# Where two weight conversions stand in the first layer's feed-forward down-projection

## What is computed

```python
FF_HIDDEN = 2816                      # D_MODEL = 1024, SEQ = 512, CTX_LEN = 256

def swiglu(h, w_i, w_o):
    g, u = jnp.split(h @ w_i, 2, axis=-1)
    return (jax.nn.silu(g) * u) @ w_o

# in second_block, for layer l, with_ctx = l < 1
xl = xl + ml[5] * rms_norm(swiglu(adaln(xl, g[2], ml[3], ml[4]), w_ffn_in[l], w_ffn_out[l]), g[3])
if with_ctx:
    xc = xc + mc[5] * rms_norm(swiglu(adaln(xc, g[2], mc[3], mc[4]), w_ffn_in[l], w_ffn_out[l]), g[3])
```

## Time and profile before

| | |
|---|---|
| median of three runs | 3219.26 us |
| profiled execution: span from first to last instruction | 3213.4 us |
| instructions in it | 44931 |
| TensorE matmul busy | 2931.1 us (91%) |
| VectorE busy | 1629.9 us (51%) |
| ScalarE busy | 1040.4 us (32%) |
| mean granted TensorE clock | 0.959 of full |

### The profile page before, as it was taken

One profiled execution on the slowest core, in us unless ns is written; L12 is line 12 of the kernel. 1 busy time (PEld: TensorE's weight loads), 2 busy tenths in 40 slices (PEclk: granted clock), 3 DMA queues, 4 the chain that ended last, 5 costly groups with the idle time before them and its releaser, 6 DMA issues.

```text
span 3213.4 us, 44931 instructions
## 1 busy us (share of the span) xinstructions
PE 2931.1 (91%) x18762; PEld 2400.9 (75%) x18762; DVE 1629.9 (51%) x3421; ACT 1040.4 (32%) x2010; POOL 208.6 (6%) x270
## 2 busy tenths in 40 slices
PE   8988999999999998888799999999899797899998
PEld 6766788888977566677568888888666686578886
DVE  4333544445445255677763433333825667654444
ACT  3223433233343245343242211211415444332222
POOL 0000000000000100100000000000211246100001
PEclk9999999999999999899899999999999798899999
DMA  7434312222222110222512212121011110223221
GB/s 234 151 111 156 103 53 60 60 60 60 73 86 105 53 33 1 83 80 80 192 59 92 66 53 66 53 77 65 36 52 33 30 41 1 92 92 105 92 96 62
DMA packets 227830, 248.75 MB, mean 77 GB/s; under 512 B 5569, under 2 KB 193069, under 8 KB 226093
## 3 DMA queue, kind: packets, MB, share of 16 engines
q1 hardware_dynamic: 227628, 245.89, 23.8%
HBM read 236.43 MB, written 9.44 MB: 77 GB/s over the span
## 4 chain that ended last, share of the span: by engine, by line
PE 56%; DVE 9%; ACT 4%; issue 2%; DMA 1%; POOL 0%; ACTq 0%; SPq 0%; DVEq 0%; POOLq 0%
PE PS L2176 52%; PE PS L2180 2%; PE PS L2386 1%; ACT AR L179 1%; DVE AR L3153 1%; ACT L174 1%; DVE STAT L3089 1%; DMA WR<-in_w_in 1%; DVE AR L2898 1%; ACT EX L179 0%; DVE AR L2913 0%; DVE EX L3140 0%; DMA WR<-in_w_mod 0%; DVE AR L2909 0%; ACT STAT L179 0%
## 5 line engine op out<-in xcount | busy, mean ns | idle before, releaser
L2176 PE MATMUL PS<-HI,WC 128*128 128x512 f32 (+2 forms) x1600 | 428.0, 353 | 0.6 <-DVE WC L3134 0.6
L2176 PE MATMUL PS<-AR 128*64 128x64 f32 (+8 forms) x3756 | 315.7, 268 | 65.5 <-ACT AR L179 24.9
L2176 PE MATMUL PS<-DW,DH 128*128 128x384 f32 (+1 forms) x1344 | 355.4, 346 | 1.0 <-ACT DH L179 1.0
L2176 PEld LDWEIGHTS PS<-AR 128*64 128x64 f32 (+5 forms) x3756 | 270.7, 171 | 111.9 <-issue 33.8
L179 ACT ACTIVATE AR<-PS 128x512 f32<-128x512 f32 (+4 forms) x389 | 165.9, 453 | 552.6 <-PE PS L2176 428.2
L2176 PEld LDWEIGHTS PS<-HI,WC 128*128 128x128 f32 x1600 | 284.0, 189 | 42.5 <-DVE WC L3134 1.1
L2176 PE MATMUL PS<-LO,WC 128*128 128x512 f32 (+2 forms) x800 | 282.2, 353 | 0.0
L2176 PE MATMUL PS<-HT,WR 128*128 128x256 f32 (+1 forms) x928 | 261.4, 435 | 15.1 <-ACT EX L179 5.7
L2176 PE MATMUL PS<-WR,HT 128*128 128x128 f32 (+2 forms) x1296 | 252.0, 352 | 11.7 <-ACT AR L179 5.4
L2176 PEld LDWEIGHTS PS<-DW,DH 128*128 128x128 f32 x1344 | 240.6, 191 | 9.7 <-issue 7.1
L179 ACT ACTIVATE EX<-PS 128x256 f32<-128x256 f32 (+2 forms) x158 | 67.7, 431 | 530.6 <-PE PS L2176 530.6
(11 more groups left out here) (444 smaller groups left out, 4991.7 us busy)
## 6 DMA issues: line engine op xcount, KB each, us to landing
WR<-in_w_ffn_in SPq DMA_DIRECT2D x40, 1024.0 KB, 6.5
WR<-in_w_in_b SPq DMA_DIRECT2D x51, 512.0 KB, 6.0
WR<-in_w_mod SPq DMA_DIRECT2D x12, 2048.0 KB, 8.1
WR<-in_w_mod SPq DMA_DIRECT2D x24, 1024.0 KB, 5.3
WR<-in_w_ffn_out SPq DMA_DIRECT2D x22, 1024.0 KB, 4.9
WR<-in_w_in SPq DMA_DIRECT2D x40, 512.0 KB, 5.2
WR<-in_w_out SPq DMA_DIRECT2D x8, 2048.0 KB, 12.3
WR<-in_w_in SPq DMA_DIRECT2D x4, 2048.0 KB, 7.7
```

What stands on the lines that cost most here:

```text
L2176: mm = lambda o, l, r, start, stop: e.o.matmul(o, l, r, start=start, stop=stop, skip_group_check=True)
```

## The change

In layer 0 (`both`), a `down` step with c = 0 issues no conversion any more. A `down` step with c = 1 issues two: one ahead of its first group, as before, and one ahead of group i = 3. The order of the conversions among themselves, their buffers and their transfers stay. Steps `up` and all of layer 1 stay as they were. This concerns the ten pairs of blocks 0 to 9. Block 10's down-projection stands in another branch, in which nothing changes; its own two weight conversions are issued in the pair of block 9, and so are among the moved ones.

```diff
@@ -2100,11 +2100,15 @@
             convert(*work[3])
-            at_ = 4
+            next_at = [4]
+            def convert_next():
+                next_at[0] += 1
+                if next_at[0] <= len(work):
+                    convert(*work[next_at[0] - 1])
             for kind, b, c in sched[2:]:
-                if kind != "act" and at_ < len(work):
-                    convert(*work[at_])
-                    at_ += 1
+                turns = () if kind == "act" else (0,) if kind == "up" or not both else ((), (0, 3))[c]
+                if 0 in turns:
+                    convert_next()
                 if kind == "up":
...
                     for i in range(nt):
+                        if i and i in turns:
+                            convert_next()
                         down(i, c, b, o, ready, ac, an)
```

## The result

The changed kernel took 3201.36 us in the median of six runs (3200.87 to 3207.97), the kernel before 3218.44 us in the median of six (3212.48 to 3229.38). The ratio is 0.9946, with a 95% interval from 0.9933 to 0.9959: it is faster, by 17.1 us between the medians. I had forecast 12.0 us less and 3202.3 to 3213.3. The direction is right, but the time lies 0.9 us under the range, so the forecast missed. What follows shows that the pairs gave the 12 us to the tenth, and that the gain comes back to about 12 us when both kernels are run more often.

The account below looks back on a forecast made before the run. TensorE, waiting for VectorE's sums, was taken to bound the ten pairs. A gain of 1.28 less 0.08 us a pair, times ten, is 12.0: 3219.3 - 12.0 = 3207.3 us, range 3202.3 to 3213.3.

Parts of the forecast that it names:

- What bounds the stretch: Ten pairs, 1768 to 2253 us: TensorE sets the time, busy 476.85 of 485 us; weight loads waited 22.3 for VectorE's sums.
- The rule for VectorE's queue: Pricing of orders in the pairs: next VectorE instruction starts 0.60, 0.33 or 1.14 us on; a group costs about 1.365.
- The first half, 8.67 us: Pair's first half without its conversion: 8.19 + 0.12 + 0.37 us, groups 5 and 6 late; gain 1.28.
- The second, 8.35: Pair's second half with two conversions: 8.19 us plus 0.08 for each, a loss of 0.08.
- What else moves: Around the moved conversions: weights done before the up-projection at 1887.3, ScalarE's copies not late, no transfer issued by them.
- The sum of 12.0 us: Ten pairs: 1.28 - 0.08 = 1.20 us gained for each, 12.0 in all.
- the median of the runs is 5.86 above the span, so 3219.3 - 12.0: Whole kernel: profiled span 3213.4 us, run median 5.86 above it, so the forecast time is 3207.3.
- may move the time by 2 or 3 us: Behind the pairs: shifts of a few low-clock stretches either way, 2 or 3 us, counted in the range.
- Only the first wait goes: Rival, first half: later waits stay at 0.16, 0.16 and 0.37 us; gain 9 us, 3210.3; chance 0.09 (within 0.3%).
- No overlap on VectorE in the new order: Rival: VectorE's instructions take whole durations (0.69, 0.42, 1.23); gain 0.34 us a pair, 3.4 in all, 3215.9; chance 0.05.
- The change does nothing: Rival: waits set by something ending together with the sums, the conversion only cover; 3219 us, chance 0.03.
- Slower through the clock: Rival, behind 2253: low-clock time of about 103 us grows by 43 to about 146, ending 9.7 us (0.3%) slower; chance 0.02.

Follow-up runs that it names:

- six other orders: The change; both conversions opening the second half; both in the first; the first's behind the gating; gating spread alone; gating spread with conversions moved: 3201.36, 3214.26, 3224.69, 3206.03, 3211.20, 3199.94 us.
- The half-changed kernel: The change in the pairs of blocks 0 to 4 alone, against the kernel before: 3209.70 us against 3215.62, ratio 0.9983.
- both repeated comparisons: The changed kernel, unedited, run twice more against the kernel before: 3205.25 us against 3215.62, ratio 0.9959; 3204.82 against 3217.38, ratio 0.9958.
- the spread gating: Gating pieces behind groups 1, 3, 5 of the first half and 1 of the second, conversions ahead of second-half groups 3 and 6, against the kernel before: 3199.94 us, ratio 0.9948.

## Why the prediction was right and wrong

*What bounds the stretch: right.* TensorE, and VectorE's sums where it waits. Matmul waits for them vanished together with the subtraction ahead of the first sum.

*The rule for VectorE's queue: right.* Its constants were read from the order before (51.52), so that one is no test. For six other orders it gave pairs of 50.32 (the change), 51.4, 52.59, 50.5, 51.16 and 49.76; measured 50.32, 51.38, 52.59, 50.46, 51.17 and 49.80. The half-changed kernel mixes two of them: 50.92 on average, measured 50.91.

*The first half, 8.67 us: right*, 8.63 measured, group 5 and 6 late as said. *The second, 8.35: right*, 8.34, with a wait of 0.21 on the loads behind each conversion. *What else moves: right*; ScalarE's copies were done before VectorE asked.

*The sum of 12.0 us: right for the pairs*, and over all runs (12.7 between the medians of 38 and 17; 12.0 is 0.37% of 3217, inside the intervals of both repeated comparisons, 0.25 to 0.56% and 0.29 to 0.54%, though not of the first, 0.41 to 0.67%).

*The step that failed is the baseline and the scatter round it*: "the median of the runs is 5.86 above the span, so 3219.3 - 12.0", and with it "may move the time by 2 or 3 us". I took 5.86 us for what lies around the span. In the changed kernel's profiled execution it is 3206.71 - 3205.4 = 1.3, and in every run that lists both it is 1.3 to 1.4. So the profiled execution of before had itself taken about 3214.7 us, and the median of three stood 4.6 us above it: that was the size of the scatter, read as a constant. Sets of six differ by nearly as much (3201.36 and 3205.25 for the same changed kernel). The time came out 5.9 us under the forecast of 3207.3, and three parts add up to that: the baseline was 1.9 us too high (3219.26 against 3217.36, the median of 38), the gain over all runs is 0.7 more than 12.0, and the first six runs of the changed kernel lie 3.3 under the median of its 17. Most of the miss is therefore the luck of a set of three and a set of six. What the prediction did wrong was to allow 2 or 3 us for it, where executions of one kernel spread over 14 and medians of six differ by 4. With 1.3 us in place of 5.86 the same sum gives 3202.7. That is nearer to this set of six, but by luck again: the one profiled execution (3214.7) lies further from 3217.36 than the median of three does.

*The rivals.* Only the first wait goes: no. The loads of groups 4, 5 and 6 waited 0.30, 0.30 and 0.49 us before, and nothing, 0.20 and 0.50 now: the waits of 4 and 5 shrank, that of 6 stayed, and the half is 8.63 us long, not the 8.88 or more of this rival. No overlap on VectorE in the new order: no; the sum at 1879.17 follows the multiply of 1878.84, 0.41 us long, by 0.33. The trace does not bear out that every next operation waits for an empty pipe; what the Trainium skill's page "VectorE: DVE Perf Modes" says of it in "The DRAIN you can't avoid" doesn't hold for these neighbours, and the section itself points to another on operations that aren't held. The change does nothing: no. Slower through the clock: no. The time at the low level does move the kernel's time, but ahead of the change as well as behind, and in the kernel before as in the changed one; behind the stretch the changed kernel's three traces had less of it, not more.

**On the clock.** In 78 timings (the kernel before, the change, its half and the spread gating, each with its pairs' gain added back) the time falls as the mean granted clock rises: medians of 3225.9 us at 0.953, 3221.0 at 0.955, 3217.0 at 0.957, 3214.4 at 0.959. The Trainium skill, page "TensorE: Matmul & The Clock Gate", section "What's actually happening", calls the count of slow matmuls at a kernel's start run-variable. No run here counts those, but these do show that the mean clock of one kernel varies from execution to execution. The traces show a part of it. In all twelve the program ahead of the first pair is the same, and that pair's first multiply stands anywhere from 1766.84 to 1777.48; the time at the low level ahead of it goes from 163.8 to 191.1 us, and the two rise together (correlation 0.94, 0.39 us for each us at the low level). That the clock causes the difference is argued from these numbers and from the same 11226 matmuls being busy 7.6 us longer. I made no run that sets the clock, and what makes one execution's low stretches longer stays open.

## What to carry to other kernels

Where two PSUM banks pass results to one engine, count for each bank's turn what else stands in that engine's queue: here a 1.23 us instruction cost over a microsecond where the queue already held 1.53 us of work for each 1.365 us group, 0.08 alone among sums, and about 1.1 more where a second stood beside it. Put such work singly, with groups between. Before a gain of a few tenths of a per cent is set against a median of three, run one kernel against itself to learn how far its times spread, compare a profiled execution's span with its own time, and read the mean clock of each run.

## What was not expected

A kernel on one core, alone, spreads over 14 us (3212.48 to 3226.42) without any change. A list of starting times and two or three spacings (0.60, 0.33 and 1.14 us on VectorE) gave the pairs of all orders to 0.04 us. And the first six runs of the changed kernel looked 5 us better than its pairs, while its own profiled execution was one of the slow ones.
